# Weight tiles 96 bytes instead of 64 behind the activations, modulo 128, in each SBUF partition

## What is computed

```
u = rmsnorm(x) * (1 + scale1) + shift1            # modulation from cond @ ada_w
aq, ak, av, bq, ... , g = split_cols(u @ w_in)    # three kinds of attention and their gates
merged = gates_a * y_a + gates_b * y_b + gates_c * y_c
x = x + gate1 * (merged @ w_o)
u2 = rmsnorm(x) * (1 + scale2) + shift2
x = x + gate2 * (square(relu(u2 @ w_ff1)) @ w_ff2)
x = rmsnorm(x)
for layer in range(2):                            # second block
    h = rms_norm(x, pre_norm[layer])
    c_b, c_c, c_x, c_z, r_q, r_k, r_v, r_z = split(h @ w_in[layer])
    y_conv = c_b * causal_conv(c_c * c_x) * silu(c_z)
    y_ret = normalised(retention(rotary(r_q), rotary(r_k), r_v)) * silu(r_z)
    x = x + rms_norm(concat(y_conv, y_ret) @ w_out[layer], post_norm[layer])
```

## Time and profile before

| | before |
|---|---|
| median of three runs | 984.34 us |
| the three runs | 982.01, 984.48, 984.34 us |
| span of the profiled execution | 980.8 us |
| PE busy | 934.8 us (95%) |
| POOL busy | 739.2 us (75%) |
| DVE busy | 665.4 us (68%) |
| ACT busy | 492.7 us (50%) |
| granted TensorE clock, mean | 0.995 |

### The profile page before, as it was taken

The page is one execution under the profiler, slowest core; times in us unless marked ns, Lnnn a source line. Parts: engine busy times, 40 slices in busy tenths (PEclk is TensorE's granted clock), DMA queues, the critical chain, the costliest instruction groups (busy, mean ns, idle before and its releaser), DMA issues.

```text
span 980.8 us, 21945 instructions
## 1 busy us (share of the span) xinstructions
PE 934.8 (95%) x7758; PEld 909.3 (93%) x7758; DVE 665.4 (68%) x1097; ACT 492.7 (50%) x811; POOL 739.2 (75%) x894
## 2 busy tenths in 40 slices
PE   6999899999789999999999999999989999999996
PEld 6898789999779999999899999999988999999996
DVE  4979996765877774652566678886466666888722
ACT  3455556654346665554454455444454444544441
POOL 1486565677687999998677659999956676799973
PEclk9999999999999999999999999999999999999999
DMA  9985555646453557565354444555515444455521
GB/s 374 401 321 178 212 177 210 236 152 246 164 192 130 204 190 273 179 216 209 129 172 155 150 166 172 174 192 194 211 45 178 167 171 155 146 192 194 178 101 43
DMA packets 28222, 185.20 MB, mean 189 GB/s; under 512 B 3027, under 2 KB 5504, under 8 KB 6272
## 3 DMA queue, kind: packets, MB, share of 16 engines
q1 hardware_dynamic: 25832, 167.93, 47.5%
q10 hardware_dynamic: 2328, 16.40, 4.6%
HBM read 183.26 MB, written 1.07 MB: 188 GB/s over the span
## 4 chain that ended last, share of the span: by engine, by line
PE 74%; DVE 16%; issue 5%; ACT 3%; DMA 1%; DVEq 1%; POOL 0%; SPq 0%; POOLq 0%; ACTq 0%
PE mm L544 21%; PE mm L545 21%; PE mm L546 21%; ACT w_hi L1001 1%; PE mm L578 1%; DVE cy L1967 1%; DVE w_lo L1406 1%; PE mm L562 1%; DVE cy L1972 1%; PE ps_s L871 1%; DVE qr L1991 1%; PE ps_o L888 1%; PE ps_o L962 1%; DVE rt L1990 1%; DVE mix_lo L1936 1%
## 5 line engine op out<-in xcount | busy, mean ns | idle before, releaser
L470 POOL TENSOR_TENSOR w_lo<-raw,w_hi 128x256 fp32r<-128x256 f32 x876 | 729.7, 869 | 215.4 <-ACT w_hi L1001 212.9
L544 PE MATMUL mm<-u_hi,w_hi 128*128 128x256 f32 x1616 | 462.2, 286 | 4.6 <-issue 4.4
L545 PE MATMUL mm<-u_lo,w_hi 128*128 128x256 f32 x1616 | 449.5, 278 | 0.0
L546 PE MATMUL mm<-u_hi,w_lo 128*128 128x256 f32 x1616 | 449.4, 278 | 0.0
L1001 ACT ACTIVATE w_hi<-raw 128x1024 fp32r<-128x1024 f32 x291 | 306.2, 1058 | 144.1 <-PE mm L546 139.6
L544 PEld LDWEIGHTS mm<-u_hi,w_hi 128*128 128x128 f32 x1616 | 304.9, 189 | 12.4 <-issue 11.9
L545 PEld LDWEIGHTS mm<-u_lo,w_hi 128*128 128x128 f32 x1616 | 304.0, 188 | 2.0 <-issue 1.9
L546 PEld LDWEIGHTS mm<-u_hi,w_lo 128*128 128x128 f32 x1616 | 304.4, 188 | 0.0
L1406 DVE TENSOR_TENSOR w_lo<-raw,w_hi 128x1024 fp32r<-128x1024 f32 x72 | 103.4, 1436 | 58.0 <-ACT w_hi L1001 55.4
L544 PE MATMUL mm<-mix_hi,w_hi 128*128 128x256 f32 x256 | 71.7, 280 | 1.5 <-DVE mix_lo L1976 1.5
L545 PE MATMUL mm<-mix_lo,w_hi 128*128 128x256 f32 x256 | 71.4, 279 | 0.0
(11 more groups left out here) (292 smaller groups left out, 1331.1 us busy)
## 6 DMA issues: line engine op xcount, KB each, us to landing
raw<-weights SPq DMA_DIRECT2D x145, 1024.0 KB, 4.8
ada_raw<-ada ACTq DMA_DIRECT2D x14, 1024.0 KB, 5.3
ada_raw<-ada SPq DMA_DIRECT2D x6, 1024.0 KB, 12.4
ada_more<-ada SPq DMA_DIRECT2D x4, 1024.0 KB, 12.7
bias<-tab_scratch SPq DMA_DIRECT2D x1, 1536.0 KB, 9.3
dec<-decay ACTq DMA_DIRECT2D x1, 1536.0 KB, 8.8
x<-xT SPq DMA_DIRECT2D x1, 1024.0 KB, 9.9
out<-x SPq DMA_DIRECT2D x4, 256.0 KB, 2.3
```

Of the source, the lines that this page charges most:

```text
L470: ins = nc.gpsimd.tensor_tensor(w_lo[:, s, at], r[:, at], hi[:, at], ALU.subtract)
L544: nc.tensor.matmul(dst, wh, rhs_hi(k), start=a, stop=False)
L545: nc.tensor.matmul(dst, wh, rhs_lo(k), start=False, stop=False)
L546: i = nc.tensor.matmul(dst, wl, rhs_hi(k), start=False, stop=b)
```

## The change

The step ahead of the weight tiles becomes 16 floats (64 bytes) and the step behind them is taken out. `w_hi` and `w_lo` move up by 32 bytes, from 96 to 0 modulo 128; all other tiles stay where they were, since 32 bytes more ahead and 32 bytes less behind cancel at `vec`. Behind `u`, `m`, `h`, `mix`, `oa`, `ob` and `oc` the weights then lie 96 bytes modulo 128 instead of 64, and behind `raw` 64 instead of 32. No instruction is added, removed or moved on any engine; only the addresses of `w_hi` and `w_lo` in them differ.

```
     keep("step_raw", [P, 8])
     raw = keep("raw", [P, RAW_PAIRS, 2 * KC * P])
-    keep("step_w", [P, 8])
+    keep("step_w", [P, 16])
     w_hi = keep("w_hi", [P, SLOTS, KC * P], F32R)
     w_lo = keep("w_lo", [P, SLOTS, KC * P], F32R)
-    keep("step_vec", [P, 8])
     vec = keep("vec", [P, N_COLS])
```

## The result

| | before | after |
|---|---|---|
| median of the runs timed together | 984.41 us (982.01 to 995.34) | 999.88 us (996.62 to 1002.26) |
| ratio after to before, 95% interval | | 1.0143 [1.0102, 1.0185] |
| span of the profiled execution | 980.8 us | 1000.2 us |
| device time of the profiled execution | not listed | 1002.26 us |

The changed kernel takes 1.4% longer. (The ratio is estimated from all runs; the quotient of the two medians would be 1.0157.) The forecast was 984 us and no change, so it was wrong in direction. The time is that of the rival "the short pitch vanishes", 999 us. In the profile after, every line number behind the taken-out step is one lower, so L543 to L545 are the three matmul lines that were L544 to L546.

The account below looks back on a forecast made before the run. PE, through its three matmul lines, was taken to bound the kernel. Both paces would remain and be dealt again, with no net change from the 984.3 us median: 984 us, range 980 to 992, 8 in 10 within 974 to 1001.

Parts of the forecast that it names:

- the short pitch vanishes: Rival: every PE stretch runs at 117.8 ns or more, +15 us, 999 us; chance 0.25, all slower.
- short pitch: The faster start-to-start pace of the three matmul lines on PE, 113.3 ns, given to about 4,150 of 6,400 matmuls.
- The step that failed: Likeliest case, PE's matmuls: both paces remain and are dealt again at restarts; 984 us, range 980 to 992, chance 0.40.
- The rival's sum: PE's matmuls: 4,150 times 4.5 ns is 18.7 us, less 3.6 us hidden in convolution: +15 us; chance 0.25.
- long pitch: The slower start-to-start pace of the three matmul lines on PE, 117.8 ns, given to about 2,250 of 6,400 matmuls.
- The worse pace that it named: PE's matmuls at 120 ns instead of 117.8, giving 1,011 us; within a rival of chance 0.25.
- Its place is above all 296 to 473: Loss mainly at 296 to 473 and the first layer's w_out stage, where PE never pauses; rival's chance 0.25.
- How the pitch is picked: PE takes one of two paces, 4.5 ns apart, when it restarts after a pause, and keeps it.
- The convolution stages stay at 74 us: Both convolution stages keep 74 us, since POOL sets their time, unless the pitch passes 118 ns.
- POOL, ACT and DVE at nothing: Reads of `raw` and `w_hi`, now 64 bytes apart instead of 32, cost nothing; at worst 4.4 us of POOL's time.
- The floor of 111 ns: Lowest pace taken for PE's matmuls, from `ident` by `ones` at distance 0; everywhere, 24.8 us less on PE alone.
- The Trainium skill's rule: TensorE reads moving tile and weights through independent ports, so the offset can't matter: sum zero, 984.3 us.

Follow-up runs that it names:

- e1: Against the kernel before: padding ahead of `raw` grown, so weights lie 96 bytes behind the activations but still 32 behind `raw`; 999.65 us, ratio 1.0117.
- e3: Against the kernel before: weights moved to the same place modulo 128 as the activations, distance 0; 1005.47 us, ratio 1.0185.
- e5: Against the kernel before: weights moved to 64 modulo 128, 32 bytes behind the activations; 1000.8 us, ratio 1.0139.
- the bare stream: Kernels without the computation, PE alone running the kernel's matmuls at many distances between moving tile and weights; most blocks of 72 matmuls lasted 8.67 to 8.91 us.
- e2: Against the kernel before: everything behind `x` moved up 32 bytes, weights at 0 modulo 128, distance still 64; 983.99 us, ratio 0.9969, profiled run 990.47 us.
- e6: Against the kernel before: `w_hi` kept at distance 64, `w_lo` alone moved to 96; 1003.84 us, ratio 1.0172.
- e9: The kernel before, unchanged, profiled once more; 987.76 us.
- e11: Against the kernel before, distance 64 kept: 28 matmuls in 14 units each made as two halves of 128 columns; 988.98 us, ratio 1.0009.
- e10: Against the kernel before: weights 192 bytes modulo 256 behind the activations instead of 64; 991.89 us, ratio 1.0052.
- e12: Against the kernel before: weights at distance 192 modulo 256, and 28 matmuls each made as two halves of 128 columns; 994.32 us, ratio 1.0089.

## Why the prediction was wrong, point by point

**The step that failed** is the first of the forecast: "the only thing the trace shows of the mechanism is that one distance gives both paces and that the restart chooses", and from it that a shift "changes which restarts end at the long pitch, not the two pitches". The runs showed that the distance decides whether the short pitch exists. In kernels it is there at 64 and 192, and nowhere at 0, 32 and 96 (e1, e3, e5, and after), and their time is 999.65 to 1005.47 us where the forecast had 984; in the bare stream it was seen at 64 or distances equal to it modulo 128 alone, though in so few restarts that this adds little. That both paces were seen at one distance was no evidence that other distances have both. The trace of before held one distance for this form of matmul, so it could not tell, and the rival with all short pitches gone deserved more than 0.25.

**The rival's sum held, its terms were small.** It priced 4,150 matmuls at 4.5 ns, 18.7 us, took off 3.6 for what the convolution stages hide, and came to +15 us and 999 us. Measured: +15.3 us in spans and +15.9 us in medians with the clock's draw removed, 999.88 us for the change. But the timeline of before has some 4,700 matmuls at the short pitch, not 4,150, most went to 118.7 and not 117.8, and PE lost 22 us. That the sum is within 1 us is partly luck: more was hidden, too, about 4.5 in the convolution stages, and some in waits of the attention stage. Its long pitch of "117.8 or more" was 117.4 to 118.7. The worse pace that it named, 120 ns, is that of distance 0, at 1005 us rather than the 1,011 worked out. "Its place is above all 296 to 473" holds for the feed-forward products, which are in the stages with 3.2 and 7.5 us more, but less for w_out of the first layer, whose stage gained only 0.8. The 2.2 us of the attention stage it hadn't counted.

**How the pitch is picked** held: at a restart, kept after it. In a run of the same distance with a long feed-forward stage (e2) the two products lasted 6.1 us longer, the 6 us that the prediction had given for it. What it hadn't seen is that the three matmuls of a block share one rhythm (e6).

**The convolution stages stay at 74 us**: held, 74.3 and 74.2, with PE busy for 74.05 and 73.93 of them. At 118.7 ns PE has next to no room left there.

**POOL, ACT and DVE at nothing**: held. L469's least and median duration are 715 and 742 ns, before 716 and 743; ACT's L1000 has a median of 1054, before 1057; and e1 gives `raw` its old distance back without effect. That L469's mean fell from 869 to 853 ns may come from running less against DVE; no run tests it. DVE and POOL got idle time, not work.

**The floor of 111 ns** from `ident` by `ones` didn't carry over: at its distance, 0, the kernel's matmuls are at their worst. That form moves 128 columns, not 256, reads one pair of tiles over and over, and both are plain float32 tiles, not fp32r like `w_hi` and `u_hi`. It was no bound for these.

**The Trainium skill's rule** (page "TensorE: Matmul & The Clock Gate", section "Step-by-step: what each phase is for"), by which moving tile and weights come through ports that don't disturb each other, would have the offset cost nothing. The measurement disagrees with what was drawn from it: 1.2 to 1.9% of the kernel's time, with no instruction changed.

**What stays open**: why 64 bytes of all multiples of 32, and whether a distance near 64 has the short pitch too; why a distance of 192 modulo 256 is dealt the long pitch more often than 64; how 128, 160 and 224 do in a kernel; and what at a restart picks the pitch and behind a pause the clock. That the reads of moving tile and next weights meet there is likely, but only argued, not shown.

## What to carry to other kernels

Where one form of matmul fills the time, read its pitch from start to start in windows without a pause, not the busy share or the duration, and try the byte distance between moving tile and weights as a parameter, modulo 256 and not only modulo 128, the same for all matmuls that alternate. Count it from the sizes of all tiles in between: the streams here had another distance modulo 256 than their names say. Two paces at one setting don't show that the setting leaves the paces alone; make one run at another setting, or price the case that the better pace belongs to this setting. And compare such kernels over several runs, since what is drawn at the restarts and by the clock was worth some 6 us each here (6.1 in the feed-forward products of e2, 5.9 in the second layer of e9), together most of the effect that was to be measured.

## What the runs showed of the hardware that was not expected

- A matmul of 256 moving columns with 128 columns of 4-byte weights can repeat every 113.3 ns at a distance of 64 bytes modulo 128. At the other multiples of 8 it was steady at 116.7 to 120.0 ns in every block of the streams, with PE alone at work. For 0, 32 and 96 over a hundred stretches each in the kernels bear that out; for the rest there are four to seven restarts each.
- At 64 modulo 128 the distance modulo 256 tells how often: short in 93 of 141 stretches at 64, in 11 of 138 at 192, and in the streams in 4 of 6 and 3 of 67 restarts.
- Both pitches can be seen at 64, and each holds through 1,326 or 1,276 matmuls in 150 us once it is there. Two half matmuls, 128 + 128 or 64 + 192 columns, changed the long to the short one in 12 of 12 blocks; 192 + 64, 224 + 32 and 32 + 224 in none of 18. In place of one whole matmul, two halves cost 0.113 us more.
- Three matmuls take 340.0 ns at the short pitch and 353.3 at the long one, which are 51 and 53 steps of 6.67 ns; at the short pitch the starts of the long stretches in the trace of before fall on nearly one phase of that grid, within some 2 ns.
- Behind the first layer's end the granted clock was 0.50 for 0, 6.8, 13.7 or 17.1 us, 6.8 in the changed kernel, 17.1 in e3 and e11, 13.7 in before taken again, 0 in before at first and in e1, e2, e5, e6, e10 and e12. With 11 more matmuls in the pauses it was 1.00 in all three profiles, and the mean clock of 30 runs was 0.991 or more, where 5 of 23 runs of before had 0.982 to 0.987.
